# Gate columns of the adaptive-norm matrix weighed on VectorE and GpSimd, one TensorE sum instead of eight rounds of matmuls, and fewer small matmuls around them

## The reference, cut to what is touched

```python
c_act = jax.nn.silu(c)                                    # (1, 1024)
mod = jnp.einsum('bd,de->be', c_act, w_ada[l]) + b_ada[l] # 6 x 1024 columns
sh1, sc1, g1, sh2, sc2, g2 = [m[:, None, :] for m in jnp.split(mod, 6, axis=-1)]
h = x * (1.0 + sc1) + sh1
proj = jnp.einsum('bsd,dk->bsk', h, w_in)
z, xbc, dt_raw, q, k, v, f_raw = jnp.split(proj, SPLITS, axis=-1)
xbc = jax.nn.silu(causal_depthwise_conv(xbc, conv_w, conv_b))
dt = jax.nn.softplus(dt_raw.astype(jnp.float32) + dt_bias)
log_f = jax.nn.log_sigmoid(f_raw.astype(jnp.float32) + f_bias)
...
x = layer_norm(ALPHA * x + (1.0 + g1) * y, ...)           # g1, sh2, sc2, g2 are used later
```

## Time and profile before

| | us |
|---|---|
| median of 3 runs | 2391.92 |
| runs | 2389.5, 2391.92, 2392.78 |
| span of the profiled execution | 2389.4 |
| `stage_prepare`, from the start to the barrier behind it | 0 to 40.2 |
| `stage_streams`, PE's first to last matmul | 40.27 to 210.8 |
| first matmul of the stage behind it | 217.93 |

### The profile page before, as it was taken

One profiled execution on the slowest core, in us unless ns is written; L12 is line 12 of the kernel. 1 busy time (PEld: TensorE's weight loads), 2 busy tenths in 40 slices (PEclk: granted clock), 3 DMA queues, 4 the chain that ended last, 5 costly groups with the idle time before them and its releaser, 6 DMA issues. The chain is left out here.

```text
span 2389.4 us, 27551 instructions
## 1 busy us (share of the span) xinstructions
PE 2281.3 (95%) x9883; PEld 1089.0 (46%) x9884; DVE 816.1 (34%) x1554; ACT 652.6 (27%) x854; POOL 202.5 (8%) x239
## 2 busy tenths in 40 slices
PE   6998999979899999989996999999999999999997
PEld 4444666634567576635455333333333333333332
DVE  1411566644352463642534211111121121112216
ACT  1211222220100000001301344344443443444441
POOL 1003111100000000000300101001011011010003
PEclk8999999989899999999996999999999999999999
DMA  8344333120531231132005969999999999999997
GB/s 338 131 188 122 80 89 105 65 87 0 225 145 71 86 125 71 53 124 74 1 27 235 366 234 397 418 422 409 422 422 414 422 420 420 422 406 423 422 407 266
DMA packets 139765, 570.75 MB, mean 239 GB/s; under 512 B 12247, under 2 KB 47244, under 8 KB 88492
## 3 DMA queue, kind: packets, MB, share of 16 engines
q1 hardware_dynamic: 123584, 527.89, 55.8%
q0 software_dynamic: 6432, 21.66, 2.4%
q10 hardware_dynamic: 9676, 20.25, 2.2%
HBM read 545.57 MB, written 24.18 MB: 238 GB/s over the span
## 5 line engine op out<-in xcount | busy, mean ns | idle before, releaser
L2481 PE MATMUL banks<-expert_ring,slot_token_gate 128*64 128x512 f32 x2880 | 638.1, 595 | 5.4 <-DMA expert_ring<-in_w_up_dram 3.3
L2481 PEld LDWEIGHTS banks<-expert_ring,slot_token_gate 128*64 128x64 f32 x2880 | 202.6, 137 | 400.7 <-issue 388.3
L2412 ACT COPY expert_ring<-expert_ring 128x2048 f32 x180 | 331.8, 1896 | 73.6 <-DMA expert_ring<-in_w_gate_dram 61.8
L2481 PE MATMUL banks<-expert_ring,slot_xT_gate 128*64 128x512 f32 x1440 | 329.8, 600 | 1.6 <-issue 0.9
L2481 PEld LDWEIGHTS banks<-expert_ring,slot_xT_gate 128*64 128x64 f32 x1440 | 100.4, 138 | 189.6 <-issue 183.1
L2586 DVE TENSOR_SCALAR col_onehot<-banks,slot_gates 128x512 f32<-128x512 f32 x45 | 33.8, 750 | 402.4 <-PE banks L2481 402.2
L486 PE MATMUL banks<-hT,weight_ring 128*128 128x512 f32 x320 | 141.6, 602 | 2.3 <-PEq L2696 2.3
L2571 DVE TENSOR_TENSOR slot_token_gate<-banks,expert_bias_T 128x512 f32<-128x512 f32 x45 | 31.1, 691 | 303.5 <-PE banks L2441 303.5
L1357 PE MATMUL banks<-hT,weight_ring 128*128 128x256 f32 x512 | 115.5, 386 | 4.2 <-PEq L2696 3.3
L723 PE MATMUL banks<-hT,weight_ring 128*128 128x512 f32 x256 | 116.8, 607 | 0.0
L1073 PE MATMUL banks<-weight_ring,mix_scaled 128*128 128x512 f32 x256 | 112.4, 600 | 3.5 <-DVE mix_scaled L1111 3.5
(11 more groups left out here) (445 smaller groups left out, 2440.8 us busy)
## 6 DMA issues: line engine op xcount, KB each, us to landing
expert_ring<-in_w_gate_dram SPq DMA_DIRECT2D x128, 1024.0 KB, 16.9
expert_ring<-in_w_up_dram SPq DMA_DIRECT2D x128, 1024.0 KB, 14.3
expert_ring<-in_w_down_dram SPq DMA_DIRECT2D x128, 1024.0 KB, 10.9
weight_ring<-in_w_ada_dram SPq DMA_DIRECT2D x12, 2048.0 KB, 11.3
weight_ring<-in_w_in_dram SPq DMA_DIRECT2D x8, 2048.0 KB, 14.9
weight_ring<-in_w_ff_in_dram SPq DMA_DIRECT2D x8, 2048.0 KB, 11.1
weight_ring<-in_w_ff_out_dram SPq DMA_DIRECT2D x8, 2048.0 KB, 13.1
weight_ring<-in_w_in_dram SPq DMA_DIRECT2D x24, 512.0 KB, 6.7
```

What stands on the lines that cost most here:

```text
L2412: nc.scalar.copy(flat_ring[:, c * size:(c + 1) * size], flat_ring[:, bass.ds(source + c * size, size)])\
L2481: x = nc.tensor.matmul(ps[h * CAP:(h + 1) * CAP, bank, :], lhs[:, k % 4, (k // 4) * CAP:(k // 4 + 1) * CAP], X.ring[:, m, k, h * HALF:(h + ...
```

## The change

Three things change in the two stages.

- The sixteen one-column matmuls that turn rows into columns, in `stage_prepare` and in `gate_cols`, become four 128x128 transposes each.
- `narrow` makes dt and f with the 32 columns of `w_dtf` as the stationary operand, in four column groups side by side, each summing two of the eight depth chunks. ACT copies the result (`part`), and four small matmuls with a folding matrix (`narrow_tokens`) add the four groups and turn them to tokens. The running sums move from behind block 3 to behind block 4.
- PE no longer reads the `ada2` chunks. DVE multiplies columns 0 to 2047 of each chunk by its column of `c_act` and adds them up in `weighed`, POOL does the same with columns 2048 to 4095, in two instructions and in place. After block 18 PE sums `weighed` over its partitions in eight matmuls (`gate_sums`). A ring slot that held an `ada2` chunk is free when both engines have weighed it. Bias and one are added to the rows before they are spread, so that POOL's two large instructions at the end go.

```diff
...
     def load(self, sp, keys):
...
             if n >= RING:
-                sp.wait_ge(self.used, n - RING + 1)
+                held = self.plan[n - RING][0]
+                if held[0] == "ada2":
+                    sp.wait_ge(self.weighed, held[1] + 1)
+                    sp.wait_ge(self.weighed2, held[1] + 1)
+                else:
+                    sp.wait_ge(self.used, self.uses(held))
...
-            for n in range(16):
-
-                j, seg = n // 4, n % 4
-                m = nc.tensor.matmul(ps[:, j, n:n + 1], mod_rows[32 * j:32 * j + 1, seg * P:(seg + 1) * P],
-                                     G.ones[32 * j:32 * j + 1, 0:1], start=True, stop=True)
+            for seg in range(4):
+                m = nc.tensor.transpose(ps[:, 0, seg * P:(seg + 1) * P], mod_rows[:, seg * P:(seg + 1) * P], G.ident[:])
             m.then_inc(cols_done, 1)
...
+            for k in range(KB):
+                G.W.wait(pool, ("ada2", k))
+                w, total = G.W.view(("ada2", k))[:, 0, 2 * D:], weighed[:, 2 * D:]
+                if k == 0:
+                    nc.gpsimd.tensor_scalar(total, w, G.c_act[:, 0:1], None, ALU.mult).then_inc(G.W.weighed2, 1)
+                else:
+                    nc.gpsimd.tensor_scalar(w, w, G.c_act[:, k:k + 1], None, ALU.mult).then_inc(weigh_step, 1)
+                    pool.wait_ge(weigh_step, k)
+                    pool.wait_ge(G.W.weighed2, k)
+                    nc.gpsimd.tensor_tensor(total, total, w, ALU.add).then_inc(G.W.weighed2, 1)
...
             def narrow():
+
                 pe.wait_ge(G.dtf_in, 16 * 5)
+                for r in range(2):
+                    for g in range(4):
+                        m = nc.tensor.matmul(ps[32 * g:32 * g + 32, 7, :], G.w_dtf[:, 2 * g + r, :], G.hT[:, 2 * g + r, :],
+                                             start=(r == 0), stop=(r == 1))
+                m.then_inc(part_done, 1)
...
+            def gate_sums():
+
+                pe.wait_ge(G.W.weighed, KB)
+                pe.wait_ge(G.W.weighed2, KB)
                 for b in range(2):
                     for j in range(4):
                         c0 = b * 2048 + j * HALF
...
+                        m = nc.tensor.matmul(ps[32 * j:32 * j + 1, 4 + b, :], G.ones[:, 0:1], weighed[:, c0:c0 + HALF],
+                                             start=True, stop=True)
+                m.then_inc(gates_done, 1)
...
                 nc.tensor.nop().then_inc(G.W.used, 1)
-                if c < 4:
-                    gate_chunk(2 * c)
-                    gate_chunk(2 * c + 1)
...
+            def weigh(k):
+
+                G.W.wait(dve, ("ada2", k))
+                w, total = G.W.view(("ada2", k))[:, 0, 0:2 * D], weighed[:, 0:2 * D]
+                if k == 0:
+                    nc.vector.tensor_scalar(total, w, G.c_act[:, 0:1], None, ALU.mult).then_inc(G.W.weighed, 1)
+                else:
+                    dve.wait_ge(G.W.weighed, k)
+                    nc.vector.scalar_tensor_tensor(out=total, in0=w, scalar=G.c_act[:, k:k + 1], in1=total,
+                                                   op0=ALU.mult, op1=ALU.add).then_inc(G.W.weighed, 1)
...
-                if n == 3:
+                if n == 4:
                     sums()
-
-            dve.wait_ge(G.W.used, G.W.index[("ada2", KB - 1)] + 1)
+                if n in (1, 2, 5, 6, 9, 10):
+                    weigh((1, 2, 5, 6, 9, 10).index(n))
+
+            weigh(KB - 2)
+            weigh(KB - 1)
...
```

More of the change, by code:

```diff
@@ L103, in __init__ @@
         self.used = ctx.enter_context(nc.semaphore("weights_used"))
+        self.weighed = ctx.enter_context(nc.semaphore("gate_rows_weighed"))
+        self.weighed2 = ctx.enter_context(nc.semaphore("gate_rows_weighed_pool"))
         self.value, count = [], [0] * RING
@@ L119, in wait, with uses @@
         pe.wait_ge(self.landed[n % RING], self.value[n])
+    def uses(self, key):
+        return sum(c[0][0] != "ada2" for c in self.plan[:self.index[key] + 1])
     def load(self, sp, keys):
@@ L323, in _ @@
             dve.wait_ge(cols_done, 1)
[L324 to L330, removed]
+            turned = ps[:, 0, :].rearrange("p (s j c) -> p j s c", j=4, c=32)[:, :, :, 0]
+            for m in range(2):
+                nc.vector.scalar_tensor_tensor(out=mod_col[:, KB * m:KB * m + KB].rearrange("p (j s) -> p j s", s=4),
+                                               in0=turned[:, 2 * m:2 * m + 2, :], scalar=float(m),
+                                               in1=G.pcol[:, R_SH1 + KB * m:R_SH1 + KB * m + KB]
+                                               .rearrange("p (j s) -> p j s", s=4),
+                                               op0=ALU.add, op1=ALU.add).then_inc(mod_ok, 1)
+            dve.wait_ge(mod_ok, 2)
             for k in range(0, KB, 2):
@@ L358, in stage_streams @@
         gates = sb("gate_rows", [P, 2, HALF])
-        bg = sb("gate_bias", [P, 2, D])
+        bg = sb("gate_bias_rows", [P, HALF])
+        weighed = sb("gate_weighed", [P, 4 * D])
+        part = sb("dtf_parts", [P, S])
+        fold = sb("dtf_fold", [P, 32])
         f_done, f_read, conv_acc, conv_free = sem("f_done"), sem("f_read"), sem("conv_acc_ok"), sem("conv_free")
@@ L385, in _ @@
             nc.gpsimd.memset(mul[:, 16:32], -1.0).then_inc(pads, 1)
+            nc.gpsimd.memset(gates[:], 0.0).then_inc(pads, 1)
             for m, c0 in ((0, 2 * D), (1, 5 * D)):
-                pool.dma_start(bg[:, m, :], A["b_ada"][0:1, c0:c0 + D].to_broadcast([P, D])).then_inc(G.gate_bias_in, 16)
+                for h in range(2):
+                    q = 64 * m + 32 * h
+                    pool.dma_start(bg[q:q + 1, :], A["b_ada"][0:1, c0 + h * HALF:c0 + (h + 1) * HALF])\
+                        .then_inc(G.gate_bias_in, 16)
+            for k in range(KB):
[8 more added lines that the diff above has]
+                    nc.gpsimd.tensor_tensor(total, total, w, ALU.add).then_inc(G.W.weighed2, 1)
             pool.wait_ge(g_rows, 8)
@@ L393, in _ @@
                     nc.gpsimd.partition_broadcast(G.gate[:, m, h * HALF:(h + 1) * HALF],
[L394 to L399, removed]
+                                                  gates[q:q + 1, 0, :]).then_inc(g_all, 1)
         @block.scalar
@@ L405, in _ @@
             nc.scalar.activation(mul[:, 0:16], G.head_rows[:, 32:48], ACT.Exp).then_inc(rate_ok, 1)
+            act.wait_ge(part_done, 1)
+            nc.scalar.copy(part[:], ps[:, 7, :]).then_inc(part_ok, 1)
             act.wait_ge(mag_ok, 1)
@@ L436, in narrow, with narrow_tokens @@
                 pe.wait_ge(G.dtf_in, 16 * 5)
+                for r in range(2):
[3 more added lines that the diff above has]
+                m.then_inc(part_done, 1)
+            def narrow_tokens():
+                pe.wait_ge(part_ok, 1)
+                pe.wait_ge(fold_ok, 1)
                 for t in range(T):
-                    for k in range(KB):
-                        m = nc.tensor.matmul(ps[:, 7, t * 32:t * 32 + 32], G.hT[:, k, t * P:(t + 1) * P],
-                                             G.w_dtf[:, k, :], start=(k == 0), stop=(k == KB - 1))
+                    m = nc.tensor.matmul(ps[:, 6, t * 32:t * 32 + 32], part[:, t * P:(t + 1) * P], fold[:],
+                                         start=True, stop=True)
                 m.then_inc(dtf_done, 1)
@@ L444, in gate_cols @@
                 pe.wait_ge(g_rows, 8)
[L445 to L450, removed]
+                for seg in range(4):
+                    m = nc.tensor.transpose(ps[:, 6, seg * P:(seg + 1) * P], gates[:, 1, seg * P:(seg + 1) * P], G.ident[:])
                 m.then_inc(gcols, 1)
-            def gate_chunk(k):
-                G.W.wait(pe, ("ada2", k))
-                w = G.W.view(("ada2", k))
+            def gate_sums():
+                pe.wait_ge(G.W.weighed, KB)
+                pe.wait_ge(G.W.weighed2, KB)
                 for b in range(2):
@@ L491, in _ @@
                         narrow()
-                    if n == 3:
+                    if n == 2:
+                        narrow_tokens()
+                    if n == 4:
                         sums()
+                    if n == FB - 2:
+                        gate_sums()
                     if n == FB - 1:
```

43 lines of the change are left out of this document (28 added, 15 removed).

## The result

The changed kernel takes 2364.52 us (median of 4 runs, 2360.7 to 2368.13) against 2390.71 for the kernel before: 0.9887 of it, 95% interval 0.9875 to 0.99, which is 24 to 30 us less (26.2 by the medians). The long wait for `z 0` didn't come.

The account below looks back on a forecast made before the run. PE, busy for 95% of the span, was taken as the bound. Savings of 23.9 us, less 14.6 waiting for `z 0` and 2.3 of clock loss, gave −7.0: 2391.9 to 2384.9 us, range 2368 to 2394.

Parts of the forecast that it names:

- The long wait for `z 0`: In front of block 13, PE would stand idle from 127.8 until `z 0` landed at 142.4: 14.6 us.
- All four go ahead of weighing 3: In `stage_streams`, POOL's chunks `ada2 2` to `ada2 5`, 39.6 us, would precede DVE's weighing 3, which would end at 133.3.
- the prediction's other prices: At the shared port from 81: POOL 9.9 us a chunk, DVE 2.74 a conv and 2.26 a weighing, added in full.
- about one turn between two POOL instructions: At the shared port, DVE would get about one instruction in between two of POOL's.
- The hold-up: At the port DVE and POOL share, whichever issues first holds it for its whole instruction; conv instructions about 5 us, not 0.75.
- the port doesn't bind: In `stage_streams`, POOL's one-input instructions leave the port free or are shorter; `z 0` lands at 121, 2368.0 us; chance 0.20.
- What a late `z 0` costs: At block 13, landing at 142.4 costs 14.6 us of PE idle time and 2.3 for the lower clock behind it.
- The terms of PE: PE's savings: `narrow` 5.4, clock behind it 2.3, gates 12.2, `gate_cols` 1.8, earlier block 1 2.2 us.
- A cost that I had at nothing: In PE's first two stages, a clock that falls elsewhere than behind the `z 0` wait was priced at nothing.
- 23.9: Up to the barrier behind `stage_streams`, the us that PE would save in all, before any waits.
- x_dt_end: Behind the barrier, it would end at about 226.4, before L634's start at 226.88; up to 7 us at risk, none taken.

Follow-up runs that it names:

- one conv later: Changed kernel with DVE's weighings of `ada2 2` and `ada2 3` behind convs 6 and 7 instead of 5 and 6: 2365.91 us, no difference.
- two convs: Changed kernel with DVE's weighing 3 behind conv 8 instead of conv 6: 2373.85 us, ratio 0.9923.
- three convs: Changed kernel with DVE's weighing 3 behind conv 9 instead of conv 6, weighings 4 and 5 one conv later: 2381.97 us, ratio 0.996.
- the old columns: Changed kernel with the sixteen one-column matmuls back in `stage_prepare`, and `mod_col`'s four additions on DVE: 2367.74 us.
- the gates on PE: Changed kernel with weighing and `gate_sums` undone, PE multiplying the `ada2` chunks again; new transposes and `narrow` stay: 2378.43 us, ratio 0.9941.
- the second profile: Profile from running the changed kernel's same file once more: 2365.48 us, ratio 0.989.
- DVE alone: Changed kernel with POOL's weighing loop gone and DVE weighing all 4096 columns: 2364.8 us, no difference.

## Why the prediction was wrong, by its steps

- **The step that failed is "All four go ahead of weighing 3".** It took the port as busy without a pause from 81 to 133, with POOL's chunks `ada2 2` to `ada2 5` all in front. The runs show three things in its place. First, the pause: `ada2 4`, which the same paragraph had landing at about 109, can't be weighed before. POOL is done with `ada2 2` and `ada2 3` at 100.8, and DVE's 10.1 of convs 5 and 6 and weighings 2 and 3 fit into the 9 that follow, up to one overlap of 1 (L415's 6.66). Weighing 3 ends at 110.9 with two chunks in front of it, not four.
- **The pause alone would not have been enough by the prediction's other prices.** 81 + 19.8 + 12.7 = 113.5 is later than 109, so weighing 3 and three instructions of conv 6 would still have met `ada2 4`, and by one turn each gone behind both chunks. So, second, the port's work doesn't add up in full: POOL's four instructions from 80.24 to 100.77 took 20.5 against 19.8 by the prices, though conv 4 (2.74 by itself) and the sums got through beside them. Third, "about one turn between two POOL instructions" is too few. In `ada2 5`'s chunk DVE's first SCALAR_TENSOR_TENSOR took 4.08, the next two 0.75 each around the end of POOL's TENSOR_SCALAR, and L593 4.74 under its TENSOR_TENSOR: four instructions, a whole conv, to a chunk of 10.4, where I had two. The run with one conv later rests on that: there weighing 3 did meet `ada2 4`, and `z 0` was in time all the same. No run takes the pause away. An estimate from the four turns, 2.6 us each: the ten instructions of convs 5 and 6 and weighings 2 and 3 would take 26 instead of 10.1, weighing 3 would end at about 127, and `z 0` would be late by about as much as in the run with two convs (6.13 of idle time), less than half of the 14.6.
- **The hold-up was right as a mechanism**, and right for POOL's one-input instruction, which no row had shown: L593's 3.95 from 82.01 ends at 85.96, 0.3 behind the end of the L415 that had begun before it. The Trainium skill ("SBUF — State Buffer", section "Who interferes with whom") says that whoever issues first holds the pair for the whole instruction. The trace agrees there, and in part elsewhere: the SCALAR_TENSOR_TENSOR of 4.08 from 121.59 ended at 125.7, 1.2 before the recorded end of the L415 that held it (126.87).
- **Rival "the port doesn't bind"** gave 2368.0, the nearest time, by a mechanism that the runs refute: convs beside POOL take twice to five times as long. What it priced is right, that no load is late.
- **What a late `z 0` costs was right**: 14.6 and 2.3 were forecast for a load that lands at 142.4; in the run with three convs it landed at 142.2, and PE lost 12.45 and 2.5. One reading there was wrong and changes nothing: the 0.69 of the earlier trace rows is the clock over the barrier's own 7.1 us, not behind it; from 217.93 to 220.93 it was 0.50. The 2.3 came from the 32 passes.
- **The terms of PE.** `narrow` with its folding takes 1.85 + 0.81 = 2.7 (2.8 forecast); block 2 takes 6.97 at clock 1.00, so 2.2 come back there (2.3); undoing both costs 8.5 to 9.5 by the medians and 7.3 in the profile (7.7). `gate_sums` takes 1.82 (1.8), and the gates are worth 11.5 in the profile (12.2). `gate_cols` takes 0.44 (0.7). Block 1 starts 2.35 earlier (2.2), but not all of that is the transposes: the 4.50 of L308 stood at a granted clock of 0.50, and in the run with the old columns the same matmuls took 2.47 at 1.00, so that block 1 started only 1.2 later than in the changed kernel.
- **A cost that I had at nothing**: block 1 starts at 37.92 in both profiles of the changed kernel, so where the columns and the turning of x run at full clock PE is idle for 4.55 in front of it, and the clock falls for 1.8. The gain of this part is then 0.5. 23.9 − 1.8 = 22.1 is what the profile shows, 22.0; without the fall it shows 23.8.
- **x_dt_end** ended at 205.4, 9.5 behind the stage's first matmul (8.5 forecast), and L696, the L634 of before, started at once; PE's L860 stood behind its own 14.59 of L785. That cost nothing, as forecast.

The gain of the medians, 26.2 (24 to 30) and 25.3, is above the 22.0 and 23.8 of the two profiles. Both profiled executions were the slowest of their four, 3.6 and 1.8 above the medians. In the first, 1.4 of the rest lies in L785's 32 passes, 14.59 instead of 16.02, where the clock behind the barrier came back sooner. Where the rest comes from, in executions that have no profile, stays open.

## What to carry to other kernels

Before two engines' work is added up on a shared resource, lay out when each piece can start: a wait for data on one engine is a free run for the other, and here nearly all of the work in question ran in one pause of 9 us. Count a hold-up in turns from a row in which both engines are busy for long, not from a pair of instructions that met once. And look at how far the late thing is from mattering: here DVE was held up by 37 us and PE didn't notice, as weighing 3 had to stand two convs later before a load missed its block.

## What the runs showed of the hardware that was not expected

- TensorE's granted clock was 0.58 in the first 3 us of block 1 behind 4.55 of idle time (the changed kernel) and 0.70 behind 3.49 (the gates on PE); it was 1.00 behind 2.29 (the second profile) and 3.11 (DVE alone). In the first profile that took away 1.8 of the 2.35 by which block 1 had come earlier.
- The same work came at either clock in different executions: the turning of x took 3.66 at 1.00 and 5.31 at 0.68 in two profiles of one kernel. The slower piece cost nothing, as block 1 started at 37.92 behind either, and behind it the clock was 1.00 in that block.
- A DVE instruction held by POOL's TENSOR_SCALAR got through 1.2 before that instruction's recorded end, and four of DVE's 128x512 instructions fitted into one pair of POOL's.
- POOL's one-input TENSOR_SCALAR over 128x2048 takes 5.44 here, longer than its two-input TENSOR_TENSOR at 4.51. The Trainium skill ("GPSIMD Engine Reference", section 4.1) calls one-input work "roughly line-rate"; DVE's own TENSOR_SCALAR of that size took 1.28.
